# Merge stage of a hybrid decoder layer: token chunks outside, weight slices inside, and rounded up-projections

## What is computed

```python
y_ret = (o_ret.reshape(B, T, -1).astype(x.dtype) * jax.nn.silu(rg)) @ w_up_ret
...
y_swa = o_swa @ w_up_swa
merged = jax.nn.sigmoid(za) * y_ret + jax.nn.sigmoid(zb) * y_swa
x = x + g1 * (merged @ w_o)
```

## Time and profile before

| | us |
|---|---|
| median of 3 runs | 1342.3 (1341.79 to 1347.84) |
| the profiled execution's own time | 1345.16 |
| its span | 1342.2 |
| PE busy | 1217.2 (91%) |
| DVE busy | 746.9 (56%) |
| ACT busy | 507.7 (38%) |
| POOL busy | 145.4 (11%) |
| merge stage, first to last matmul | 510.38 to 802.79 |
| PE, mean granted clock | 0.958 of 2.4 GHz |

### The profile page before, as it was taken

The page is one execution under the profiler, slowest core; times in us unless marked ns, Lnnn a source line. Parts: engine busy times, 40 slices in busy tenths (PEclk is TensorE's granted clock), DMA queues, the critical chain, the costliest instruction groups (busy, mean ns, idle before and its releaser), DMA issues.

```text
span 1342.2 us, 18081 instructions
## 1 busy us (share of the span) xinstructions
PE 1217.2 (91%) x6817; PEld 937.2 (70%) x6817; DVE 746.9 (56%) x1433; ACT 507.7 (38%) x862; POOL 145.4 (11%) x166
## 2 busy tenths in 40 slices
PE   4789999999997999999999998998499999999966
PEld 1677677676775698888888877886367766666632
DVE  0855656665567342221122216447589998888828
ACT  2633423334233221111011113112288887778732
POOL 1210000000000000000000001110122233333201
PEclk9899999999998999999999998999599999999978
DMA  9542221422222122111111004234699999999754
GB/s 342 220 164 93 84 101 70 151 90 84 95 75 86 55 111 94 48 47 47 47 47 47 0 11 181 93 127 173 220 328 376 356 366 356 355 364 371 269 223 175
DMA packets 53613, 219.60 MB, mean 164 GB/s; under 512 B 7944, under 2 KB 15696, under 8 KB 44970
## 3 DMA queue, kind: packets, MB, share of 16 engines
q1 hardware_dynamic: 45138, 197.25, 40.0%
q0 software_dynamic: 7488, 18.29, 4.1%
q10 hardware_dynamic: 928, 3.28, 0.6%
HBM read 201.90 MB, written 24.72 MB: 169 GB/s over the span
## 4 chain that ended last, share of the span: by engine, by line
PE 73%; DVE 11%; DMA 9%; issue 3%; ACT 3%; SPq 1%; POOL 0%; POOLq 0%; DVEq 0%; ACTq 0%
PE p L1726 13%; PE p L1966 10%; PE p L2074 10%; DMA G<-in_we 7%; PE p L1970 6%; PE psS L1993 4%; PE psS L2093 4%; PE p L1902 3%; PE psS L1966 3%; PE p L1993 3%; PE psS L1970 2%; DMA M<-in_w_ada 1%; DVE E L1091 1%; PE psS L1778 1%; PE p L1807 1%
## 5 line engine op out<-in xcount | busy, mean ns | idle before, releaser
L1726 PE MATMUL p<-A 128*128 128x512 f32 (+3 forms) x1080 | 258.3, 386 | 12.1 <-DVE A L1102 12.1
L1726 PEld LDWEIGHTS p<-A 128*128 128x128 f32 (+1 forms) x1080 | 174.7, 182 | 63.5 <-DVE A L1102 13.8
L2074 PE MATMUL p<-C 128*96 128x512 f32 x768 | 196.8, 409 | 16.5 <-DVE C L1611 16.5
L2074 PEld LDWEIGHTS p<-C 128*96 128x96 f32 x768 | 124.4, 168 | 73.3 <-issue 24.3
L1501 DVE TENSOR_TENSOR C<-G,C 128x2048 fp32r<-128x2048 f32 x64 | 146.2, 2284 | 24.1 <-ACT C L961 23.9
L1366 DVE TENSOR_TENSOR work<-p,work 128x384 f32<-128x384 f32 (+1 forms) x36 | 18.6, 516 | 238.1 <-ACT work L892 237.6
L1966 PE MATMUL p<-A,B 128*128 128x384 f32 (+1 forms) x864 | 142.7, 323 | 2.0 <-DVE M L1299 2.0
L1966 PEld LDWEIGHTS p<-A,B 128*128 128x128 f32 x864 | 137.0, 188 | 4.5 <-issue 2.2
L961 ACT CAST C<-G 128x2048 fp32r<-128x2048 f32 x62 | 118.8, 1916 | 20.3 <-DMA G<-in_we 12.4
L2093 PE MATMUL psS<-C 128*96 128x512 f32 x384 | 97.4, 403 | 2.0 <-DVE C L1623 2.0
L1970 PE MATMUL p<-M 128*128 128x384 f32 (+1 forms) x288 | 87.2, 452 | 0.0
(11 more groups left out here) (280 smaller groups left out, 1754.9 us busy)
## 6 DMA issues: line engine op xcount, KB each, us to landing
G<-in_we SPq DMA_DIRECT2D x96, 1024.0 KB, 19.7
M<-in_w_ada SPq DMA_DIRECT2D x8, 2048.0 KB, 8.2
M<-in_x SPq DMA_DIRECT2D x18, 512.0 KB, 5.7
M<-in_rope SPq DMA_DIRECT2D x45, 192.0 KB, 2.4
D<-in_w_qkv SPq DMA_DIRECT2D x4, 2048.0 KB, 10.6
F<-in_lift SPq DMA_DIRECT2D x8, 1024.0 KB, 5.1
M<-y_dram SPq DMA_DIRECT2D x8, 1024.0 KB, 11.8
M<-in_w_ada SPq DMA_DIRECT2D x8, 768.0 KB, 9.6
```

The costliest lines, as they stand in the source:

```text
L1726: last = mm(out, x[k][:, t0:t0 + rows], y(k), start=k == 0 and j == 0, stop=k == KD - 1 and j == 2)
L2074: last = mm(up_bank[slot][0:CAP, :], x[:, k, :], kcols(w, k), start=k == 0 and j == 0, stop=k == KD - 1 and j == 2)
```

## The change

The loops change places: the three token chunks are outside, the 8 weight slices inside. Step `i` is now chunk `i // 8`, slice `i % 8`, and both weights of a slice are loaded, cast and subtracted again for every step. The up-projections are made in the split form: weights (`wy_hi`, `wy_lo`) and branch outputs (`o_hi`, `o_lo`) are rounded, and each product becomes three with rounded operands. The branch outputs are rounded by chunk (`mixed_hi`, `mixed_lo`): chunk 0 ahead of the first step, chunk 1 in step 1, chunk 2 in step 9. Gates and up-projections of a step have semaphores of their own on PE (`mg_g`, `mg_mm`) and in the loads (`lw_in`, `wy_in`); ACT casts the weights of step `i + 1` ahead of the sigmoids of step `i`, which follow the gate part. The first part of `w_o` is loaded into a place that frees up in the stage, in three loads issued in step 16. The loops of ACT, DVE and SP are written out; PE has one loop for each chunk. Several semaphores of other stages are merged into fewer (`vm_r` into `sqm`, `h_a` into `hid_r`, `x2_r`, `x2_sq`, `rs3_r` into `x1_r`, `x1_sq`, `rs2_r`), with counts that keep each wait at the same event.

The diff, cut to the stage:

```diff
@@ SP
-            lift_in(0, 0)
+            gates_in(0)
+            ups_in(0)
             sp.wait_ge(s["rg_r"], 12)
             sp.wait_ge(s["late_st"], 32)
-            lift_in(1, 1)
-            sp.dma_start(D_wp, A["w_o"][:, 0:3 * D]).then_inc(s["wo_in0"], 16)
-            with sp.Fori(1, KD // 2) as m2_:
-                for slot in range(2):
-                    sp.wait_ge(s["mg_mm"], 3 * (2 * m2_ + slot - 1))
-                    lift_in(2 * m2_ + slot, slot)
+            gates_in(1)
+            ups_in(1)
+            for i in range(2, 3 * KD):
+                sp.wait_ge(s["mg_g"], i - 1)
+                gates_in(i)
+                sp.wait_ge(s["mg_mm"], i - 1)
+                ups_in(i)
+                if i == 2 * KD + 1:
+                    for k in range(3):
+                        sp.dma_start(wo_raw[k], quarters(A["w_o"][:, k * D:(k + 1) * D])).then_inc(s["wo_in0"], 16)
@@ ACT
+            def weights_hi(i):
+
+                act.wait_ge(s[f"lw_in{i % 2}"], 16 * (i // 2 + 1))
+                if i >= 2:
+                    act.wait_ge(s["mg_g"], i - 1)
+                nc.scalar.copy(z_hi[i % 2], z_raw[i % 2]).then_inc(s["w_hi"], 1)
+                act.wait_ge(s[f"wy_in{i % 2}"], 16 * (i // 2 + 1))
+                if i >= 2:
+                    act.wait_ge(s["mg_mm"], i - 1)
+                nc.scalar.copy(wy_hi[i % 2], wy[i % 2]).then_inc(s["w_hi"], 1)
+
+            def mixed_hi(c):
+
+                c0, w0 = MC[c]
+                for j in range(2):
+                    nc.scalar.copy(o_hi[c][j], o_raw[j][:, :, c0:c0 + w0]).then_inc(s["ot_hi"], 1)
+
+            weights_hi(0)
             rg(11)
...
+            act.wait_ge(s["rg_r"], 12)
+            mixed_hi(0)
+
+            for i in range(3 * KD):
+                c, m = divmod(i, KD)
+                bz = lift[4 * (i % 2):]
+                if i + 1 < 3 * KD:
+                    weights_hi(i + 1)
+                act.wait_ge(s["mg_g"], i + 1)
+                for j in range(2):
+                    nc.scalar.activation(g2b[:, i % 2, j, 0:MC[c][1]], bz[j][:, 0:MC[c][1]], ACT.Sigmoid).then_inc(s["mg_s"], 1)
+                if m == 1 and c < 2:
+                    mixed_hi(c + 1)
@@ DVE
+            for i in range(3 * KD):
+                c, m = divmod(i, KD)
+                q, w0 = i % 2, MC[c][1]
+                by = lift[4 * q:]
+                if i + 1 < 3 * KD:
+                    weights_lo(i + 1)
+                if m == 1 and c < 2:
+                    mixed_lo(c + 1)
+                dve.wait_ge(s["mg_s"], 2 * i + 2)
+                dve.wait_ge(s["mg_mm"], i + 1)
...
@@ PE
-                    for j, src in enumerate((oretT, oswT)):
-                        for k in range(H):
-                            last = mm(bs[2 + j][:, 0:w0], wy[slot][:, (4 * j + k) * P:(4 * j + k + 1) * P], src[:, k, cols],
-                                      start=k == 0, stop=k == H - 1)
-                    last.then_inc(s["mg_mm"], 1)
+                last.then_inc(s["mg_g"], 1)
+                pe.wait_ge(s["w_lo"], 2 * i + 2)
+                for j in range(2):
+                    pe.wait_ge(s["ot_lo"], 2 * c + j + 1)
+                    for k in range(H):
+                        wc = slice((H * j + k) * P, (H * j + k + 1) * P)
+                        for n, (w, x) in enumerate(((wy_hi, o_hi[c][j][:, k]), (wy_hi, o_lo[j][:, k, cols]),
+                                                    (wy_lo, o_hi[c][j][:, k]))):
+                            last = mm(bs[2 + j][:, 0:w0], w[slot][:, wc], x, start=k == 0 and n == 0,
+                                      stop=k == H - 1 and n == 2)
+                last.then_inc(s["mg_mm"], 1)
```

More of the change, by code:

```diff
@@ L49 @@
 EMPTY = 2048
+LATE = NT + 1
 assert EMPTY >= TA and 2 * EMPTY >= 2 * TA
@@ L873, in _ @@
             rg(10)
[L875 to L882, removed]
-            rg(11)
[L885 to L894, removed]
@@ L1376, in _, with weights_lo @@
-            with dve.Fori(0, KD // 2 - 1) as m2_:
-                link.loop(m2_, 12)
-                merge(2 * m2_, 0)
-                merge(2 * m2_ + 1, 1)
-            link.end(KD // 2 - 1)
-            merge(KD - 2, 0)
-            merge(KD - 1, 1, split=False)
+            def weights_lo(i):
+                dve.wait_ge(s["w_hi"], 2 * i + 1)
+                nc.vector.tensor_tensor(z_lo[i % 2], z_raw[i % 2], z_hi[i % 2], ALU.subtract).then_inc(s["w_lo"], 1)
+                dve.wait_ge(s["w_hi"], 2 * i + 2)
+                nc.vector.tensor_tensor(wy_lo[i % 2], wy[i % 2], wy_hi[i % 2], ALU.subtract).then_inc(s["w_lo"], 1)
@@ new lines, in mixed_lo @@
+            def mixed_lo(c):
+                c0, w0 = MC[c]
+                for j in range(2):
+                    dve.wait_ge(s["ot_hi"], 2 * c + j + 1)
+                    nc.vector.tensor_tensor(o_lo[j][:, :, c0:c0 + w0], o_raw[j][:, :, c0:c0 + w0], o_hi[c][j], ALU.subtract
+                                            ).then_inc(s["ot_lo"], 1)
+            weights_lo(0)
+            rg(11)
+            mixed_lo(0)
+            for i in range(3 * KD):
[8 more added lines that the diff above has]
+                dve.wait_ge(s["mg_mm"], i + 1)
+                for j in range(2):
+                    link(nc.vector.tensor_tensor(g2b[:, q, 2 + j, 0:w0], by[2 + j][:, 0:w0], g2b[:, q, j, 0:w0], ALU.mult))
+                n = w0 // P
+                a, b = (g2b[:, q, 2 + j, 0:n * P].rearrange("p (t c) -> p t c", t=n) for j in range(2))
+                last = nc.vector.tensor_tensor(mT[:, 3 * c:3 * c + n, m, :], a, b, ALU.add)
+                if c == 2:
+                    last = nc.vector.tensor_tensor(mTs[:, m, :], g2b[:, q, 2, n * P:w0], g2b[:, q, 3, n * P:w0], ALU.add)
+                last.then_inc(s["mg_r"], 1)
@@ L1974, in _, with merge @@
-            merge(0, 0, False)
-            merge(0, 1, False)
-            with pe.Fori(1, KD // 2) as m2_:
-                merge(m2_, 0, True)
-                merge(m2_, 1, True)
+            def merge(c, m2_, slot):
+                i = KD * c + 2 * m2_ + slot
+                pe.wait_ge(s["w_lo"], 2 * i + 1)
+                if not isinstance(i, int) or i >= 2:
+                    pe.wait_ge(s["mg_r"], i - 1)
+                elif i == 0:
+                    pe.wait_ge(s["rg_r"], 12)
+                bs = lift[4 * slot:]
+                c0, w0 = MC[c]
+                cols = slice(c0, c0 + w0)
+                for j in range(2):
+                    for k in range(KD):
+                        wc = slice((KD * j + k) * P, (KD * j + k + 1) * P)
+                        for n, (w, x) in enumerate(((z_hi, hT_hi[k]), (z_hi, hT_lo[k]), (z_lo, hT_hi[k]))):
+                            last = mm(bs[j][:, 0:w0], w[slot][:, wc], x[:, cols], start=k == 0 and n == 0,
+                                      stop=k == KD - 1 and n == 2)
+                last.then_inc(s["mg_g"], 1)
+                pe.wait_ge(s["w_lo"], 2 * i + 2)
+                for j in range(2):
+                    pe.wait_ge(s["ot_lo"], 2 * c + j + 1)
[6 more added lines that the diff above has]
+                last.then_inc(s["mg_mm"], 1)
@@ L1981, in project @@
+            merge(0, 0, 0)
+            merge(0, 0, 1)
+            with pe.Fori(1, KD // 2) as m2_:
+                merge(0, m2_, 0)
+                merge(0, m2_, 1)
+            for c in (1, 2):
+                with pe.Fori(0, KD // 2) as m2_:
+                    merge(c, m2_, 0)
+                    merge(c, m2_, 1)
             def project(t, slot, part, rows=P, first=False, w_new=False):
```

125 lines of the change are left out of this document (49 added, 76 removed).

## The result

The changed kernel takes 1323.88 us (median of 4 runs, 1320.44 to 1324.85) against 1342.63 us before (median of 4, 1341.79 to 1347.84). The ratio is 0.9845, with a 95% interval of 0.9819 to 0.9872. That is 18.8 us less, where 18.3 were forecast. The profiled execution took 1322.91 us, with a span of 1321.1 us.

A forecast was written before the change was run, and what follows sets the result against it. The prediction took PE's matmuls alone to bound the merge stage (292 us). Its terms, -20.5 + 1.3 + 1.6 - 0.7 = -18.3 us, gave 1324 us against the median of 1342.3; the 8-in-10 range was 1319 to 1333.

The forecast's parts named there:

- Rounded up-projections, -20.5 us: Merge stage: 24 rounded matmuls at the gates' rate replace 8 plain ones, 4.20 us wide and 2.92 narrow; 20.5 us less.
- The rival by the ratio of passes: Up-projections: three rounded products cost three quarters of a four-pass plain one; 27.8 us less there, 1317 us; chance 0.02.
- The rival with the rate of the weight loads: Up-projections: new matmuls run at their weight loads' 188 ns, 4.5 us an up part, about 1342 us; chance 0.03.
- The start, +1.3: Start of the merge stage: one more DVE subtraction ahead of the last gating group has no cover; 1.3 us more.
- The clock, +1.6: First merge matmuls: PE's gap of about 3.2 us lowers the clock to 1.2 GHz; 1.6 us more, bounds 0 and 2.5.
- The lower bound, 0: Start of the merge stage: the clock price if PE's gap lowers nothing, 0 us.
- Weights in each step, 0: Merge stage: fetching and rounding weights in 24 steps, not 8, is covered by matmuls; spare 7.6 us wide, 2.5 narrow; no cost.
- The formula for late loads: Merge steps: with landing time L, a narrow step loses (L - 7.5) / 2 us and a wide one (L - 12.6) / 2.
- Load of ACT and DVE, 0: Merge stage: in a narrow step of 8.75 us DVE needs under 5.3 and ACT under 4; no cost.
- w_o's first part, 0, up to 3: Step 16: w_o's loads, queued ahead of step 18's gate weights, may delay them; taken as 0, bounds 0 and about 3 us.
- The end, -0.7: End of the merge stage: the last sigmoids leave the chain, so DVE starts at once; 0.7 us less.
- The slower rival, transfers as the bound: Merge stage: late landings bound the steps; the gain is gone from L = 12.1 us, 1430 us at 19.7; chance 0.04.

The follow-up runs named there:

- experiment 1: Changed kernel with plain float32 up-projections again, keeping the new loop order and all 24 loads: 1346.75 us, ratio 1.0031 to the kernel before.
- experiment 8: Changed kernel with DVE subtracting the first up weights behind the last gating products, not ahead of them: 1322.88 us, ratio 0.9827 to the kernel before.
- experiment 7: Changed kernel with one more 128x2048 addition on DVE ahead of the last gating products, lengthening PE's gap: 1327.18 us, ratio 0.9862 to the kernel before.
- experiment 2: Changed kernel with weights loaded, cast and subtracted for the first chunk only: 1323.69 us, ratio 0.9861 to the kernel before.
- experiment 4: Changed kernel with one PE count for gates and up-projection together, given when the step is done: 1327.61 us, ratio 0.9880 to the kernel before.
- experiment 3: Changed kernel with ACT making a step's sigmoids ahead of the next step's weight casts: 1365.27 us, ratio 1.0170 to the kernel before.
- experiments 5 and 6: Changed kernel with each gate load issued three times (5) or four times (6), the cast waiting for all: 1355.02 and 1408.93 us.
- experiment 10: Changed kernel with POOL's cast of the second tile held until DVE has subtracted w_o's first part: 1323.84 us, ratio 0.9855 to the kernel before.

## Why the prediction was right, point by point

1. *Rounded up-projections, -20.5 us.* Right: 4.19 and 2.92 us an up part, a stage shorter by 20.4 us, and experiment 1 puts all of it back with this one edit. The rate of the gates' matmuls was the right price for the new ones. The rival by the ratio of passes is out: it asked for a stage 27.8 us shorter. The rival with the rate of the weight loads is out as well. One reading of mine was too strong: that the trace bears out four passes, since 645 is four times 161. No run shows a product of 161 ns; 645 is 3.7 times the 175 of a rounded one, and the trace has two records for each plain matmul.
2. *The start, +1.3.* Measured +1.14, the duration of one subtraction when it follows another without a gap; experiment 8 takes just this away. I had priced it by a mean that one slowed instruction had raised.
3. *The clock, +1.6.* Wrong in this place: behind gaps of 3.08 or 3.09 us the granted clock was 1.00 in all profiles with that gap, and the first 48 matmuls took 8.64 or 8.65 us, as behind 1.95 us before. The step that failed was to order gaps by length, between one of 2.28 us that lowered the clock and one of 5.43. The trace of the kernel before already speaks against such an order, in a row that the prediction doesn't show: a burst of 4.49 us behind 2.41 us, where the earlier trace rows has 3.00 us behind the same 2.41. The lower bound, 0, was the case. At 5.3 us the term is real and 2.1 us (experiment 7).
4. *Weights in each step, 0.* Right, and by the reason given: PE had no wait within the stage, and experiment 2 took 16 of the 24 loads away without a gain. The spare was small in the places named. In experiment 4, which gives up part of it, the narrow steps wait; in experiment 3, which gives up more, all do. The formula for late loads had threshold and slope right for the waits (experiments 5 and 6), if the landing is counted from the request. It lacked the clock, 1.0 us for each narrow step in experiment 5, and step 1, whose load has only the first step's time.
5. *Load of ACT and DVE, 0.* Right: DVE was busy 73 us more and nothing waited. But it rests on the order on ACT, as experiment 3 shows.
6. *w_o's first part, 0, up to 3.* Right at the edge: the gate load behind it landed after 6.7 us in the changed kernel's profile, and after 7.4 to 7.5 in two others, where PE lost 0.4 to 0.5 us.
7. *The end, -0.7.* Measured -0.63: the sigmoids (two of 0.39 us, overlapping) left the chain, and come back with experiment 4.

The row named in point 3, from the trace of the kernel before:

```profile
1199.41 4.49 PE L2074 MATMUL p<-C 128*96 128x512 f32 x12 [2.41 <-DVE C L1611]
```

The sum of what the traces show for these terms is +1.1 - 20.4 - 0.6 = -19.9 us, against -18.3. That the medians differ by 18.8 and the two profiled spans by 21.1 lies in the parts outside the stage, by scatter or by the change itself. So the close match of 1324 and 1323.9 is partly luck: one term of 1.6 us was not there, and 1 to 2 us more in parts that the sum doesn't cover made up for it. The slower rival, transfers as the bound, needs more than twice the traffic: with 3.5 MB a step in place of 1.5 (experiment 5) the kernel is slower than the one before.

## What to carry to other kernels

Three matmuls with rounded operands cost less here, at 384 and 264 columns, than one with plain float32 operands, as long as the rounding has cover: price them by a row of the same kernel with the same width, not by the ratio of passes. A loop order that fetches weights three times is free while landing, cast and subtraction fit between the release of a buffer and its next use; work that time out for the shortest step and for the first, count it from the request, and look at what is queued ahead of the load. On a half-idle engine, put what the bound engine needs next ahead of what it needs two steps on.

## What was not expected of the hardware

- Short gaps of PE and its clock: 3.08 or 3.09 us did not lower it in any of seven profiles at the start of the merge, where matmuls at full rate had run up to the gap. 5.29 and 5.58 us did. Between shorter gaps of one length it went both ways: 2.41 us in the expert stage (3.00 and 4.49 us for 12 matmuls), 1.95 us in experiment 3 (3.19 and 4.71 us for 24). The length of the gap alone doesn't decide; what else does is left open.
- A cast on POOL and DVE's subtractions (both 128x1024) slow each other, in a certain order. The subtraction that runs when the cast starts keeps its 1.2 us; the next one takes 2.06, and the cast 1.9 where later casts of that size take 1.04. When the cast was moved, the slow subtraction moved with it (experiment 10).
